# Gathering, adding and scattering each expert block's rows inside the expert loop, in place of a final gather-and-add stage

## The reference

```
h = h + merged @ w_out
u2 = rms_norm(h, norm2_w)
g_idx = top group of 4;  e_idx, e_val = top 2 of its 8 experts     # 2 of 32 experts per token
gate  = g_val * e_val / sum(e_val)
# the 2048 assignments are sorted by expert into blocks of 128 slots, each expert padded to full blocks
buf_t = token of each slot (n_tok for padding), buf_g = its gate (0 for padding)
hid = silu(xblk @ w_gate[e]) * (xblk @ w_up[e])
yb  = hid @ w_down[e]
y   = zeros.at[buf_t].add(yb * buf_g)
out = h + y[:n_tok]
```

## Time and profile before

| | us |
|---|---|
| median of 3 runs (lowest to highest) | 2677.85 (2671.97 to 2678.9) |
| the profiled execution | 2684.54 |
| its span | 2682.8 |

### The profile page before, as it was taken

The page is one execution under the profiler, slowest core; times in us unless marked ns, Lnnn a source line. Parts: engine busy times, 40 slices in busy tenths (PEclk is TensorE's granted clock), DMA queues, the critical chain, the costliest instruction groups (busy, mean ns, idle before and its releaser), DMA issues. The chain is left out here.

```text
span 2682.8 us, 65515 instructions
## 1 busy us (share of the span) xinstructions
PE 2538.7 (95%) x27857; PEld 2170.3 (81%) x27857; DVE 1548.3 (58%) x2352; ACT 1307.8 (49%) x2252; POOL 342.6 (13%) x345
## 2 busy tenths in 40 slices
PE   6999999999999999989999999999998999999992
PEld 5888898877777776788988998888888888888882
DVE  4566665443055655544444444563326999999994
ACT  4655462322134444434444444562223788888871
POOL 0112112331000000001212221200000111111102
PEclk9999999999999999999999999999999999999996
DMA  4354243222133224122222201153355999999976
GB/s 114 129 184 155 99 168 126 83 91 79 44 101 95 67 85 169 39 57 68 63 56 60 61 22 34 49 157 119 128 188 222 391 417 414 413 414 413 413 314 267
DMA packets 163345, 440.41 MB, mean 164 GB/s; under 512 B 16944, under 2 KB 97522, under 8 KB 150794
## 3 DMA queue, kind: packets, MB, share of 16 engines
q1 hardware_dynamic: 147081, 381.91, 39.8%
q10 hardware_dynamic: 9088, 29.49, 2.7%
q0 software_dynamic: 6912, 25.17, 2.4%
HBM read 344.18 MB, written 92.34 MB: 163 GB/s over the span
## 5 line engine op out<-in xcount | busy, mean ns | idle before, releaser
L2691 DVE TENSOR_TENSOR ex_wL<-wx,ex_wH 128x2048 fp32r<-128x2048 f32 x192 | 436.2, 2286 | 47.0 <-ACT ex_wH L2595 43.8
L2595 ACT CAST ex_wH<-wx 128x2048 fp32r<-128x2048 f32 x192 | 366.3, 1911 | 108.7 <-PE ex_bank L2483 84.3
L2481 PE MATMUL ex_bank<-ex_wH,ex_xTH 128*128 128x512 f32 x512 | 202.9, 396 | 0.6 <-DVE ex_xTL L2696 0.6
L2483 PE MATMUL ex_bank<-ex_wL,ex_xTH 128*128 128x512 f32 x512 | 200.4, 391 | 0.0
L2482 PE MATMUL ex_bank<-ex_wH,ex_xTL 128*128 128x512 f32 x512 | 199.8, 390 | 0.0
L728 PE MATMUL ph_acc<-ph_wH,uH 128*128 128x512 f32 (+1 forms) x416 | 167.3, 402 | 0.0
L420 PE MATMUL pf_acc<-uH,pf_wH 128*128 128x348 f32 x648 | 160.6, 356 | 6.4 <-DVE pf_wL L542 6.4
L728 PE MATMUL ph_acc<-ph_wH,uL 128*128 128x512 f32 (+1 forms) x416 | 164.4, 395 | 0.0
L728 PE MATMUL ph_acc<-ph_wL,uH 128*128 128x512 f32 (+1 forms) x416 | 163.7, 393 | 0.0
L2458 POOL DMA_INDIRECT ex_x<-s_u,ex_idx x32 | 70.6, 2205 | 584.3 <-PE ex_bank L2489 444.0
L420 PE MATMUL pf_acc<-uL,pf_wH 128*128 128x348 f32 x648 | 138.7, 323 | 0.0
(11 more groups left out here) (417 smaller groups left out, 6877.6 us busy)
## 6 DMA issues: line engine op xcount, KB each, us to landing
wx<-in_expert_w_gate SPq DMA_DIRECT2D x32, 2048.0 KB
wx<-in_expert_w_up SPq DMA_DIRECT2D x32, 2048.0 KB
wx<-in_expert_w_down SPq DMA_DIRECT2D x32, 2048.0 KB
s_y<-ex_y ACTq DMA_DIRECT2D x32, 512.0 KB, 10.5
fw<-in_w_in SPq DMA_DIRECT2D x27, 512.0 KB, 21.3
hw<-in_w_in SPq DMA_DIRECT2D x40, 256.0 KB
mb_gt<-s_pT SPq DMA_DIRECT2D x16, 512.0 KB, 3.5
s_y<-pf_zero SPq DMA_DIRECT2D x15, 512.0 KB, 6.0
```

Source lines behind the costliest of these rows:

```text
L2481: nc.tensor.matmul(out, aH, bH, start=first, stop=False)
L2483: return nc.tensor.matmul(out, aH, bL, start=False, stop=last)
L2595: nc.scalar.copy(wH[:, w, part], raw(j, s)[:, part]).then_inc(w_high, 1)
L2691: nc.vector.tensor_tensor(wL[:, w, part], raw(j, s)[:, part], wH[:, w, part], ALU.subtract).then_inc(w_low, 1)
```

## The change

- `output_and_route` stores h into the output tensor `out` itself, and the token numbers start at 1024 (`tid` base SEQ), so that a slot without a token reads 0 in the product PI.
- `route` makes from PI two index lists: `idx`, the token (0 for padding), for gathers, and `to`, the token or a number beyond the bound for padding, for scatters. Such rows are left out by the scatter (`bounds_check`).
- The gates go to the slots by a second product PS = here x (block one-hot times gate), in a high and a low part, 32 matmuls ahead of the dummy matmuls.
- The activation is Silu instead of Sigmoid, and `mix` is one product instead of two.
- ScalarE no longer copies and stores y. VectorE adds instead (`add_y`): the rows of `out` that block n belongs to, plus y(n) from PSUM times the share of each slot. `project(n)` on TensorE waits for add_y(n-1).
- GpSimd gathers these rows (`rows`), and scatters them back after the add (`scatter`), waits until the scatter has landed, and only then gathers the rows of the next block.
- VectorE's loop is written out instead of a loop instruction.
- The stage `combine`, the load of h, the stores of zeros, `yD`, `h2D` and `sidx` are gone.

```diff
 # project_recurrent: SP
-                if n == 8:
-                    sp.wait_ge(zeroed, 1 + OPEN)
-                    for x in range(NE, NBLK):
-                        sp.dma_start(c.yD[x * SLOTS:(x + 1) * SLOTS, :], zero[:]).then_inc(cleared, 16)
...
 # output_and_route: SP
-                sp.dma_start(c.h2D[t], h[:, s, :]).then_inc(h_out[s], 16)
+                sp.dma_start(c.out[0, t * TS:(t + 1) * TS, :], h[:, s, :]).then_inc(h_out[s], 16)
...
 # experts: GpSimd
+            def rows(n):
+                pool.indirect_dma_start(y[:, n % 2, :], None, c.out[0], bass.IndirectOffsetOnAxis(ap=idx[:, n:n + 1], axis=0)).then_inc(rows_in, 16)
+
+            def scatter(n):
+                pool.wait_ge(y_added, n + 1 + OPEN)
+                pool.indirect_dma_start(c.out[0], bass.IndirectOffsetOnAxis(ap=to[:, n:n + 1], axis=0), y[:, n % 2, :], None,
+                                        bounds_check=SEQ - 1, oob_is_err=False).then_inc(scattered, 16)
+                pool.wait_ge(scattered, 16 * n + 16)
+
             pool.wait_ge(idx_ready, 1 + OPEN)
+            gather(0)
+            gather(1)
+            pool.wait_ge(share_split, 1 + OPEN)
+            pool.wait_ge(to_ready, 1 + OPEN)
+            rows(0)
+            for n in range(2, 4):
+                pool.wait_ge(x_turned, n - 1 + OPEN)
+                gather(n)
             for n in range(NE):
-                if n >= 2:
-                    pool.wait_ge(x_turned, n - 1 + OPEN)
-                gather(n)
+                if n + 4 < NE:
+                    pool.wait_ge(x_turned, n + 3 + OPEN)
+                    gather(n + 4)
+                scatter(n)
+                if n + 1 < NE:
+                    rows(n + 1)
...
 # TensorE, project(n) and place
-            pe.wait_ge(y_moved, n + OPEN)
+            pe.wait_ge(y_added, n + OPEN)
...
             last.then_inc(found, 1)
+            pe.wait_ge(share_split, 1 + OPEN)
+            for n in range(2 * NS):
+                nc.tensor.matmul(PS, here[:, n, :], shH[:, n, :], start=(n == 0), stop=False)
+                last = nc.tensor.matmul(PS, here[:, n, :], shL[:, n, :], start=False, stop=(n == 2 * NS - 1))
+            last.then_inc(shared, 1)
...
 # ScalarE
-                nc.scalar.activation(sg[:], bank[:, GATE_BANK[s], :], ACT.Sigmoid).then_inc(opened, 1)
+                nc.scalar.activation(sg[:], bank[:, GATE_BANK[s], :], ACT.Silu).then_inc(silu, 1)
...
-                    move_y(s, n, i, rank(DN, n))
...
 # VectorE
-                nc.vector.tensor_tensor(hid[:], bank[:, GATE_BANK[s], :], sg[:], ALU.mult).then_inc(silu, 1)
-                dve.wait_ge(silu, n + 1 + OPEN)
                 dve.wait_ge(w_used, 2 * r + 2 + OPEN)
-                nc.vector.tensor_tensor(hid[:], bank[:, UP_BANK, :], hid[:], ALU.mult).then_inc(mixed, 1)
+                nc.vector.tensor_tensor(hid[:], bank[:, UP_BANK, :], sg[:], ALU.mult).then_inc(mixed, 1)
+
+            def add_y(n, r):
+                dve.wait_ge(w_used, 2 * r + 2 + OPEN)
+                dve.wait_ge(rows_in, 16 * n + 16)
+                row = y[:, n % 2, :].rearrange("p (o f) -> p o f", o=2)
+                nc.vector.scalar_tensor_tensor(out=row, in0=bank[:, 5:7, :], scalar=share[:, n:n + 1], in1=row,
+                                               op0=ALU.mult, op1=ALU.add).then_inc(y_added, 1)
...
-                nc.vector.tensor_copy(idx[:], PI).then_inc(idx_ready, 1)
-                ch(nc.vector.tensor_copy(c.sidx[:].rearrange("p j t -> p (j t)"), sf[:, 0, :]))
+                ts(idx[:], PI, float(SEQ), -float(SEQ), ALU.max, ALU.add).then_inc(idx_ready, 1)
+                gates = c.gate[:].rearrange("p j t -> p (j t)")
+                per = lambda a: a.unsqueeze(2).to_broadcast(two)
+                ch(nc.vector.tensor_copy(gH, gates))
+                ch(tt(gL, gates, gH, ALU.subtract))
+                ch(tt(shH, blk, per(gH), ALU.mult))
+                ch(tt(shL, blk, per(gL), ALU.mult))
+                dve.sem_inc(share_split, 1)
+                ch(ts(pad[:], PI, 1.0, 4.0 * SEQ, ALU.is_lt, ALU.mult))
+                nc.vector.scalar_tensor_tensor(out=to[:], in0=PI, scalar=-float(SEQ), in1=pad[:],
+                                               op0=ALU.add, op1=ALU.add).then_inc(to_ready, 1)
...
+            dve.wait_ge(share_ready, 1 + OPEN)
+            for n in range(NE - 2):
+                s = n % 2
+                low_h(n)
+                for h in range(2):
+                    low(U, 1 - s, h, rank(U, n + 1), s)
+                low_x(s, n + 2)
+                for h in range(2):
+                    low(G, s, h, rank(G, n + 2), 1 - s)
+                add_y(n, rank(DN, n))
+                low(DN, 1 - s, 0, rank(DN, n + 1), s)
+                mix(1 - s, n + 1, rank(U, n + 1))
+                low(DN, 1 - s, 1, rank(DN, n + 1), s)
...
-def combine(nc, c):
```

More of the change, by code:

```diff
@@ L287, in _ @@
             tt = nc.gpsimd.tensor_tensor
-            nc.gpsimd.memset(zero[:], 0.0).then_inc(zeroed, 1)
             for p in range(NF):
@@ L2346, in experts @@
         idx = sb("ex_idx", [SLOTS, NB2], U32)
+        to = sb("ex_to", [SLOTS, NB2], U32)
+        pad = sb("ex_pad", [SLOTS, NB2])
+        share = sb("ex_share", [SLOTS, NB2])
         inc = sb("ex_inc", [128, NE])
@@ L2366, in experts @@
         x_turned, x_high, x_low = sem("ex_x_turned"), sem("ex_x_high"), sem("ex_x_low")
-        opened, silu, mixed = sem("ex_opened"), sem("ex_silu"), sem("ex_mixed")
+        silu, mixed = sem("ex_silu"), sem("ex_mixed")
         h_turned, h_high, h_low = sem("ex_h_turned"), sem("ex_h_high"), sem("ex_h_low")
-        y_moved = sem("ex_y_moved")
-        y_out = [sem(f"ex_y_out{s}") for s in range(2)]
+        y_added = sem("ex_y_added")
         block = begin()
@@ L2406, in experts @@
         there = wL[:, 1, 2 * NS * SLOTS:2 * NS * (SLOTS + NB2)].rearrange("p (n b) -> p n b", b=NB2)
+        shH, shL = (wH[:, 1, h * 2 * NS * NB2:(h + 1) * 2 * NS * NB2].rearrange("p (n b) -> p n b", b=NB2) for h in range(2))
+        gH, gL = (wH[:, 1, 4 * NS * NB2 + h * 2 * NS:4 * NS * NB2 + (h + 1) * 2 * NS] for h in range(2))
         M_, GSUM, GI, M1, I1, M2, I2, DF, E2, DEN = range(10)
@@ L2475, in overflow @@
                     gather(n + NE)
+                    rows(n + NE)
+                    scatter(n + NE)
                     overflow(n + 1)
@@ L2676, in overflow @@
                     move_h(n + NE)
-                    move_y(0, n + NE, n + NE // 2, r + 2)
-                    act.wait_ge(y_out[0], 16 * (n + NE // 2 + 1) + OPEN)
-                    act.sem_inc(over_stored, 1)
                     overflow(n + 1)
             overflow(0)
-            for s in range(2):
-                act.wait_ge(y_out[s], 16 * NE // 2 + OPEN)
         @block.vector
@@ L2806, in _ @@
                 low(G, 0, h, 0, 0)
+            dve.wait_ge(shared, 1 + OPEN)
+            nc.vector.tensor_copy(share[:], PS).then_inc(share_ready, 1)
             low_x(0, 0)
@@ L2815, in _ @@
             low(DN, 0, 1, rank(DN, 0), 1)
-            with dve.Fori(0, NE // 2 - 1) as i:
-                for s in range(2):
-                    n = 2 * i + s
-                    low_h(n)
-                    for h in range(2):
-                        low(U, 1 - s, h, rank(U, n + 1), s)
-                    low_x(s, n + 2)
-                    for h in range(2):
-                        low(G, s, h, rank(G, n + 2), 1 - s)
-                    low(DN, 1 - s, 0, rank(DN, n + 1), s)
-                    mix(1 - s, n + 1, rank(U, n + 1))
-                    low(DN, 1 - s, 1, rank(DN, n + 1), s)
+            dve.wait_ge(share_ready, 1 + OPEN)
[11 more added lines that the diff above has]
+                low(DN, 1 - s, 1, rank(DN, n + 1), s)
             n = NE - 2
@@ L2836, in _ @@
             spill(ch)
+            add_y(n + 1, ORANK - 1)
             used = dve.alloc_register("ex_dve_used")
@@ L2851, in overflow @@
                     low_h(n + NE)
+                    add_y(n + NE, r + 2)
                     overflow(n + 1)
             overflow(0)
-def combine(nc, c):
-    with ExitStack() as st:
-        sb, ps, sem, begin = scope(nc, st)
-        h = c.wx[1][:, 0:2].rearrange("p a w -> p (a w)").rearrange("p (n d) -> p n d", d=D)
-        y = sb("co_y", [TS, NS, 2, D])
-        y_in = [sem(f"co_y_in{t}", 0) for t in range(NS)]
-        half = sem("co_half")
-        summed = sem("co_summed")
-        out = sem("co_out")
-        block = begin()
-        @block.gpsimd
-        def _(pool):
-            for t in range(NS):
-                for j in range(2):
-                    pool.indirect_dma_start(y[:, t, j, :], None, c.yD,
-                                            bass.IndirectOffsetOnAxis(ap=c.sidx[:, j, t:t + 1], axis=0)).then_inc(y_in[t], 16)
-        @block.vector
-        def _(dve):
-            for t in range(NS):
-                dve.wait_ge(y_in[t], 32)
```

(11 more changed lines are left out.)

32 lines of the change are left out of this document (8 added, 24 removed).

## The result

| | us, median (lowest to highest), runs |
|---|---|
| before | 2674.48 (2671.81 to 2678.9), 5 |
| after | 2761.81 (2750.87 to 2767.69), 5 |

The change makes the kernel slower: ratio 1.0325 with a 95% interval of 1.0306 to 1.0344, 87 us. The forecast was 2709 in a range of 2648 to 2790. The profiled execution of after took 2750.87 with a span of 2749.1, 66.3 above the span before.

The account below looks back on a forecast made before the run. TensorE, never waiting in the expert loop, was taken as the bound, with VectorE and DMA nearly full. Loop +64 and outside -33 (end -38, zero stores -1, front +6) gave +31 on the median 2677.85: 2709 us, range 2648 to 2790.

Parts of the forecast that it names:

- Which value: Expert loop: step that summed issues, landings, add and semaphores of the scatter-gather chain to 20.0 us a block, against 17.73.
- the value holds itself: Expert loop: a shorter chain closes the weight-load gap and slows the scatter, a longer one widens it; block stays 20.0 us.
- nearer 5 than 10: Expert loop, sign of being wrong: landing of the rows' gathers nearer 5 us than 10; forecast took 10.5.
- 28 periods: Expert loop: all blocks but the first two and last three are stretched, by 2.3 us each, +64 us.
- rival 3: Expert loop: stopped TensorE loses its clock; if that adds to the chain, blocks of 21.7 us, 2756 us; chance 0.09.
- The end: After the last projection: 44.3 us shrink to 6.3 for add, scatter issue, landing and closing, a gain of 38 us.
- 7 to 8: End of the span, sign in the changed trace: 7 to 8 us from the last projection to the end.
- some 0.9 us of semaphores and closing: End of the span: allowance of some 0.9 us within the 6.3 us left after the last projection.
- The front: Ahead of the loop: share split, 32 matmuls and dummies make the first turn of tokens 6 us later.
- +64 - 33 = +31: Whole kernel: loop +64 us, net outside the loop -33 us, together 31 us slower.
- Rival 1: Expert loop: chain stays hidden or nearly so, blocks of 17.73 to 18.6 us, 2645 to 2669 us; chance 0.34.
- the three: Rival 1, rival 3 and a second: both transfers beside weights throughout, blocks 22 to 27.4 us, 2765 to 2916; chance 0.08.

Follow-up runs that it names:

- experiment 1: Changed kernel, but from block 2 on each weight load brings a quarter of its bytes, chain untouched: 2658.82 us, ratio 0.9912 to the kernel before.
- experiment 4: Changed kernel with the four groups' blocks in turn, rows gathered two blocks ahead, padding left out: 2726.34 us, ratio 1.0173 to the kernel before.
- experiment 8: Changed kernel, groups in turn, scatter adding in DRAM, no rows gathered, no GpSimd wait for landings, dummies moved, one drain: 2655.40 us, ratio 0.9889 to before.
- experiment 3: Changed kernel, but the gather of rows leaves out padding slots: 2780.35 us, ratio 1.0376 to the kernel before.
- 9: As experiment 8, but token gathers from block 2 on leave out padding slots: 2663.16 us, ratio 0.9913 to the kernel before.
- 7: As experiment 4, but the token gather is issued behind the scatter, ahead of the wait for its landing: 2689.04 us, ratio 1.0032 to the kernel before.

## Why the prediction was right in direction and too small

**Right: the mechanism and its side.** The chain of scatter, landing, rows and add sets the block, it is long only beside weights (experiment 1), and TensorE, VectorE and the DMA engines all show gaps. DMA share 0.91 against the forecast's 0.9.

**Wrong: the step "Which value".** It gave the block 0.94 + 4.5 + 2.33 + 10.5 + 1.7 = 20.0 us and argued that "the value holds itself". Scatters are 21.2 us apart on average ((2644.88 - 2114.69) / 25), and that average is a middle between two kinds of block, long ones (24.1) and short ones (18.55). A long block, from the rows above: 2.25 issue + 10.03 landing + 1.55 issue + 9.63 landing up to the add + 2.11 for the add and its semaphores = 25.57. A short one, 2327.97 to 2347.10: 2.25 + 2.48 + 3.08 + 5.55 landing + 3.67 in which the rows are there and VectorE is not + 2.11 = 19.1. Its pace is TensorE's, which frees the buffers for the casts. The gap that I had put into each block comes every other block, whole. By terms, as means of the 25 periods:
- landing of the scatter: 5.5 (138.6 / 25, the waits above) against 4.5, +1.0;
- its issue: 2.25 against 0.94, +1.3. I had taken the shorter of the two issues in the earlier trace rows for an instruction that takes 2.25 in each block here, even in experiment 1 with a DMA share of 0.50. In experiment 4, right behind two other issues, it took 1.0 (median), so what sets it is open;
- issue of the rows' gather: 2.2 against 2.33, -0.1;
- its landing: 7.5 against 10.5, -3.0. The 10.5 nearly held in long blocks (9.5) and not in short ones (5.7). My own sign of being wrong, "nearer 5 than 10", is met in 13 of 25 blocks;
- rows that lie ready before VectorE comes: 1.6 (3.0 in short blocks), for which the sum had no term, +1.6;
- the add up to the next scatter: 2.1 against 1.7, +0.4.

Together 21.2, the average block; so 20.0 was as near as that only because the landing of the rows, taken too long, made up for four terms taken too short or left out. The count was right: 28 periods stretched by 21.2 - 17.73 = 3.5 are 97 of the 98.2 us. The miss in the loop, +34 us, is 1.2 us a block in this one step.

**Wrong: rival 3 was kept apart.** The text said that a lower clock changes nothing "as long as the chain runs beside it". It does run beside it in long blocks, but not in short ones, which are TensorE's own: they take 18.55 on average, 0.8 above 17.73. TensorE's time in the loop is made up so: 500 us hold 500 / 21.2 = 23.6 blocks of 17.73 us at full clock = 418; TensorE was busy 441, so 23 us, 1.0 us a block, are slow matmuls, and 59 us, 2.5 a block, are standing. This is not what a full clock would give back: long blocks last as long as their chain does. No run separates the clock's part from the chain's.

**The terms outside the loop.** The end was to give 38 and gave 30.5. From the last projection to the end it took 14.6 us, not the 6.3 of the sum or the "7 to 8" of the signs; the scatter's issue and landing were as forecast (1.01 us and under 3.3), but GpSimd's drain of 7.90 us behind it was in the sum only as a part of "some 0.9 us of semaphores and closing". The trace of before had one of 2.67 us (shown above), so a term was due, though not its size. The front was to cost 6 and cost 10.5: the forecast took the 32 products at the pace of the earlier trace rows (4.5 us) although it had just made TensorE stand 2.7 us, and the earlier trace rows showed what a stand of 2.47 us does to the clock. At half the clock they took 6.8 and the dummies 2 more. Together +12 of the miss.

So +64 - 33 = +31 became +98 - 20 = +78 in the two profiles, when the 12 us of an index that came early by chance are left out; the medians have +87. What makes up the last 9 us is open; executions of after spread over 17 us.

**What was right by luck.** TensorE's busy share came out as forecast (0.88 against 0.89) by two errors: blocks of 21.2 us with matmuls at full clock would give 0.84, and slow matmuls count as busy. Rival 3's sum (chain and clock, 2756) was 6 us from the result, but it had blocks of 20.0 + 1.7 us, each alike, which no row shows. The range held the result.

**Which rival was near.** None of the three was the case as told. Rival 1's block of 17.73 us is what experiment 1 shows, and experiment 8 in its first half. The outside gives 32 us in experiment 8, where the drain and the dummy matmuls are moved, close to the forecast's 33; as the change was made it gives 20.

## What to carry to other kernels

A transfer that nobody waits for has no price in a profile; price it, when something is made to wait for it, by the landing of the same size beside the same traffic, and take the issue time from the loop too. If a chain stops the engine whose loads make the traffic, long and short periods can take turns, as here; price both, not a middle. Before a gather, add, scatter chain, ask for the order of work in which neighbours share no rows and let the scatter add: here that costs 10 us in the loop instead of 98 (experiment 8). And count the drain at the end of a kernel whose GpSimd has issued many DMAs.

## What the runs showed of the hardware

- From the end of its issue, a scatter of 128 rows of 4 KB (about half of them written) lands in 2.5 to 3.5 us when the last weight load was asked for 7.4 us or more before, and in 5.5 to 10.7 when it was asked for 3.6 us before (25 periods of after); where the weights hardly stop, plain or adding ones land 14 to 16 us after the start of their issue (medians of experiments 4, 7 and 8).
- A gather of 128 rows of 4 KB lands 5.7 us after its issue in the short blocks of after and 9.5 in the long ones (means).
- The issue of a plain scatter takes 2.25 us in the loop of after, 1.01 at the end of its span and 1.0 at the median of experiment 4; an adding one 1.5 to 3.7; a gather 0.9 to 3.1.
- Leaving out padding rows by the bound made neither the landing (experiment 3) nor the loop (9) faster.
- GpSimd's closing drain takes 0.62 us after 7 indirect DMAs, 2.67 after 32, 5.28 after 64, 7.90 after 96. A drain inside the loop, with DMAs in flight, took 8.6 to 27.8 us.
